# Feed-forward up projection: the raw weights' last product moved to the fourth place, and GpSimd's tables held back while VectorE makes its sums

## The chip, the core and the metric

One core of a Trainium2 chip runs the whole program. The metric is device time in microseconds (us) of one execution. Of the kernel before, three executions took 1297.13, 1298.35 and 1299.34 us; their median, 1298.35 us, is the time that the changed kernel is compared with.

## The reference, cut to what matters

The program computes one transformer block with a gated linear attention mixer and a convolutional gated feed-forward part, and then a second block (attention and delta-rule mixers, and 32 experts of which each token uses two). Everything is float32, with 256 tokens and a model width of 1024. The change touches only the feed-forward part of the first block:

```python
def conv_ffn(x, w_up, conv_w, conv_b, w_down):
    s = x.shape[1]
    u = x @ w_up                                   # [256, 1024] x [1024, 2 * 2816]
    u_pad = jnp.pad(u, ((0, 0), (CONV_WIDTH - 1, 0), (0, 0)))
    u = sum(u_pad[:, j:j + s] * conv_w[j] for j in range(CONV_WIDTH)) + conv_b
    gate, up = jnp.split(u, 2, axis=-1)
    return (jax.nn.silu(gate) * up) @ w_down       # [256, 2816] x [2816, 1024]
```

## The kernel before, in words

**How the up projection is tiled.** The hidden width of 2816 is cut into 22 tiles of 128 gate columns and 128 up columns. Each tile is a matrix product split two by two in three directions: the 256 tokens into halves, the 1024 inputs into a top and a low half, and the columns into gate and up. A scheme in Strassen's manner makes it from seven products of 128 x 512 by 512 x 128 instead of eight. Each product is four TensorE matmuls in the program and eight in the trace (float32 takes two passes). The profile calls the line of all of them L712.

**The seven products of tile i, in the order before.** X (raw gate weights, written to the PSUM bank `UP_X`); the corner, which belongs to tile i-1 and is added onto bank `UP_Q`; Y (raw weights, bank `UP_Y`); X1 (a table, added onto `UP_X`); Q (a table, bank `UP_Q`); X2 (a table, added onto `UP_X`); Z (raw up weights, bank `UP_Z`). Tile 0 has no corner. After each of X, X1 and X2 ScalarE copies bank `UP_X` to SBUF (copies 0, 1 and 2, lines L1380, L1386, L1388), and the next product that writes that bank waits for the copy. There is one such bank, so that X of the next tile waits for copy 2 of this one. VectorE adds the copies to banks `UP_Q`, `UP_Y` and `UP_Z` (L1774), does the convolution's taps (L1737) and the gate's multiplication (L1748); ScalarE does the first tap (L1364) and the silu (L1370).

**Where the operands come from.** SyncE's queue (SP) loads a tile's weights, 1 MB, into one of two buffers (L448). Load i waits until tile i-2 has used the buffer: for TensorE's product count `up_done` and for the four tables of that tile. After loads 4, 7, 10, 13 and 16 a 2 MB chunk of another matrix (`w_ada`, L228) goes through the same queue. GpSimd (POOL) makes four sums of weight quarters for each tile, the tables (L2267 to L2272), and in the down projection four for each of its 11 pairs of tiles (L2280 to L2285). VectorE makes four sums of token quarters once, `tok_sums` (L1726 to L1731), and four for each pair of the down projection (L1756 to L1759).

**The down projection** makes 7 products of 128 x 128 by 128 x 512 for each pair (L781): p1, p2, p6, p7, p5, p4, p3. Of pair 0, p6 waits for VectorE's sums and GpSimd's tables, and p4 for a small VectorE step, `modulation(1, 7, 8)` (L1767), which stands behind the sums of pair 1 in VectorE's order. The first such step, `modulation(0, 1, 0)`, frees the bank that Z of tile 0 writes.

All orders are written out by hand; each engine runs its list in order, and semaphores tie the lists together.

Of the kernel before, what the change touches and what calls it, by code (L numbers as in the profile page):

```python
# [104 lines left out]
def build_program(nc, I, out):  # L105

    ctx = ExitStack()
    with ctx:
# [271 lines left out]
        for group, steps in (  # L380
# [5 lines left out]
            ("pool_tables", (("vr_tables", 8), ("up_tables", 4 * FT), ("down_tables", 4 * NPAIR), ("x2_part", 3))),  # L386
# [43 lines left out]
        def _(sp):  # L430
# [100 lines left out]
        def _(pe):  # L531
# [190 lines left out]
            def ff_up(i, s, loaded, first=False):  # L722
# [16 lines left out]
                pe.wait_ge(*after("up_tables", i * 4 + 2))  # L739
                pe.wait_ge(S["up_copied"], i * 3 + 1)  # L740
                up_product(UP_X, up_t[s][:, 1], tok_sums[:, 1], False)
                if not first:
                    pe.wait_ge(S["up_added"], i * 4)
                up_product(UP_Q, up_t[s][:, 0], tok_sums[:, 0], True)
                if first:
                    pe.wait_ge(*after("tok_sums", 3))
                pe.wait_ge(*after("up_tables", i * 4 + 3))
# [10 lines left out]
            def ff_down(p):  # L758
# [7 lines left out]
                for name in PART:  # L766
# [27 lines left out]
            pe.wait_ge(*after("up_tables", 4 * FT))  # L794
# [505 lines left out]
        def _(act):  # L1300
# [71 lines left out]
            def up_copies(i, s, first=False, taps_free=None):  # L1372
# [249 lines left out]
        def _(dve):  # L1622
# [105 lines left out]
            dve.tensor_tensor(tok_sums[:, 1], quarters[1][1], tok_sums[:, 0], ALU.subtract).then_inc(made("tok_sums"), 1)  # L1728
            dve.tensor_tensor(tok_sums[:, 2], quarters[1][1], quarters[0][1], ALU.subtract).then_inc(made("tok_sums"), 1)
            dve.wait_ge(*after("tok_sums", 3))  # L1730
            dve.tensor_tensor(tok_sums[:, 3], tok_sums[:, 1], quarters[1][0], ALU.subtract).then_inc(made("tok_sums"), 1)  # L1731
# [29 lines left out]
            def modulation(group, b, plain):  # L1761

                dve.wait_ge(S["ada_turned"], group + 1)
                turned = bank(b).rearrange("p (n r) -> p n r", n=16)[:, :, 0]
                bias = col("b_ada")[:, 16 * group:16 * group + 16]
                for n0 in (0, 8):
                    m = dve.scalar_tensor_tensor(out=mod[:, 16 * group + n0:16 * group + n0 + 8], in0=turned[:, n0:n0 + 8],  # L1767
                                                 scalar=0.0 if n0 == plain else 1.0, in1=bias[:, n0:n0 + 8], op0=ALU.add, op1=ALU.add)
                m.then_inc(S["mod_ready"], 1)

            modulation(0, 1, 0)
# [4 lines left out]
            def up_adds(i, s, first=False):  # L1776
# [11 lines left out]
                dve.wait_ge(S["up_done"], i * 7 + 6)  # L1788
# [456 lines left out]
        def _(pool):  # L2245
# [15 lines left out]
            pool.wait_ge(S["rows_scaled"], 4)  # L2261
            for i in range(FT):
# [4 lines left out]
                pool.tensor_tensor(t[:, 0], w[:, 0:4, 1, :], w[:, 4:8, 1, :], ALU.add).then_inc(made("up_tables"), 1)  # L2267
                pool.wait_ge(*after("up_tables", 4 * i + 1))
# [108 lines left out]
```

## Time and profile before

| | |
|---|---|
| median of 3 runs | 1298.35 us (1297.13 to 1299.34) |
| the profiled execution's own time | 1298.34 us |
| its span on the core | 1296.5 us |
| busy in the span: TensorE matmul | 1145.4 us (88%) |
| VectorE | 487.1 us (38%) |
| ScalarE | 246.1 us (19%) |
| GpSimd | 237.2 us (18%) |
| mean granted TensorE clock | 0.971 of full speed |

The up projection stands between about 170 and 318 us of the span, the down projection between 318 and 390 us. In the trace a row is a group of like instructions: start, length, engine, line, operation, output<-inputs with shapes, and in brackets how long the engine had been idle and whose work ended that. PE is TensorE's matmul, PEld its weight load, DVE VectorE, ACT ScalarE, POOL GpSimd, SPq SyncE's queue. A matmul's length is its latency. Matmuls are pipelined and start much closer together than that.

### The profile page before, as it was taken

Reading aid. Unit: us, or ns where it says so; the run is one execution under the profiler, and the core shown is the slowest. Engines: PE = TensorE matmul, PEld = TensorE weight load, DVE = VectorE, ACT = ScalarE, POOL = GpSimd, SP = SyncE. Lnnn points to the kernel's source line nnn. Section 1 sums busy time; section 2 is a strip of 40 time slices with the busy share of each in tenths; the row PEclk is TensorE's granted clock in tenths of the full one; section 3 lists DMA queues with packets and bytes.
Section 4 is the critical chain, followed back from the end, with each engine's and each line's share of the span. In section 5 each row is a group of like instructions: output and inputs, shape, how many; then the busy total and the mean of one; then the engine's idle time right before and its main releaser. Section 6 shows DMA issues by size and latency. Waiting matters only on the chain.

```text
span 1296.5 us, 22618 instructions
## 1 busy us (share of the span) xinstructions
PE 1145.4 (88%) x8992; PEld 801.6 (62%) x8993; DVE 487.1 (38%) x1093; ACT 246.1 (19%) x561; POOL 237.2 (18%) x160
## 2 busy tenths in 40 slices
PE   7999989998999999999998999877887667788766
PEld 5646489998448878888858985533444323444333
DVE  2213155567663623442574312422332212333224
ACT  1302023333002211054201201211111101111112
POOL 0550066888770000000102000300000000000000
PEclk9999999999999999999998999989999879999889
DMA  9338737653347454431444096599999999699996
GB/s 333 139 129 316 276 123 292 240 214 129 134 142 240 130 195 146 179 131 65 103 153 136 1 349 239 205 380 403 431 429 428 428 429 428 259 429 429 429 428 264
DMA packets 88169, 334.86 MB, mean 258 GB/s; under 512 B 24353, under 2 KB 25505, under 8 KB 72882
## 3 DMA queue, kind: packets, MB, share of 16 engines
q1 hardware_dynamic: 72850, 331.94, 65.2%
q10 hardware_dynamic: 15264, 2.13, 1.0%
q8 instruction: 41, 0.67, 0.2%
q14 instruction: 14, 0.11, 0.0%
HBM read 332.22 MB, written 1.84 MB: 258 GB/s over the span
## 4 chain that ended last, share of the span: by engine, by line
PE 72%; DMA 17%; DVE 4%; issue 4%; ACT 1%; SPq 1%; POOL 0%; DVEq 0%
PE ps L544 18%; DMA main<-in_w_up 11%; PE ps L1211 9%; PE ps L712 9%; PE ps L781 5%; PE ps L554 4%; PE ps L598 4%; PE ps L1228 3%; DMA main<-in_w_gate 3%; PE ps L1097 2%; DMA main<-in_l_ffn_w_up 2%; PE ps L1191 2%; PE ps L1164 1%; PE ps L974 1%; DMA main<-in_l_gla_w_in 1%
## 5 line engine op out<-in xcount | busy, mean ns | idle before, releaser
L1211 PE MATMUL ps<-main 128*32 128x256 f32 x2176 | 176.9, 414 | 79.2 <-issue 38.0
L544 PE MATMUL ps<-main 128*128 128x256 f32 x1088 | 239.0, 381 | 0.6 <-DMA main<-in_l_gla_w_in 0.6
L544 PEld LDWEIGHTS ps<-main 128*128 128x128 f32 x1088 | 207.1, 191 | 32.6 <-issue 3.4
L1211 PEld LDWEIGHTS ps<-main 128*32 128x32 f32 x2176 | 90.8, 119 | 164.5 <-issue 110.3
L712 PE MATMUL ps<-main 128*128 128x128 f32 x1232 | 141.9, 278 | 5.1 <-DMA main<-in_l_ffn_w_up 2.8
L712 PEld LDWEIGHTS ps<-main 128*128 128x128 f32 x1232 | 140.1, 194 | 7.0 <-issue 4.5
L2176 DVE TENSOR_TENSOR main<-main,ps 64x256 f32<-64x256 f32 x34 | 14.4, 423 | 200.9 <-ACT main L1575 125.5
L781 PE MATMUL ps<-main 128*128 128x512 f32 x154 | 68.2, 605 | 3.6 <-DVE main L1759 3.6
L1228 PE MATMUL ps<-main 128*32 128x256 f32 x1088 | 65.8, 381 | 5.1 <-ACT main L1581 4.0
L1888 DVE SCALAR_TENSOR_TENSOR main<-ps,cols,main 128x255 f32<-128x255 f32 (+2 forms) x72 | 33.0, 480 | 69.7 <-ACT main L1437 68.0
L554 PE MATMUL ps<-main 128*128 128x512 f32 x128 | 55.6, 594 | 1.1 <-DVE main L1971 0.6
L781 PEld LDWEIGHTS ps<-main 128*128 128x128 f32 x154 | 29.7, 194 | 41.4 <-issue 36.7
L1164 PE MATMUL ps<-main 128*32 128x256 f32 x560 | 42.5, 389 | 12.0 <-DMA main<-in_w_up 8.3
L1575 ACT ACTIVATE main<-ps 64x256 f32<-64x256 f32 x34 | 12.8, 377 | 210.4 <-PE ps L1211 210.4
L1228 PEld LDWEIGHTS ps<-main 128*32 128x32 f32 x1088 | 36.2, 109 | 25.5 <-issue 11.7
L2295 POOL TENSOR_TENSOR main<-main,consts 128x2048 f32<-128x2048 f32 x1 | 4.5, 4533 | 247.5 <-DVE main L1968 247.5
L2267 POOL TENSOR_TENSOR main<-main 128x512 f32<-128x512 f32 x22 | 28.6, 1299 | 109.3 <-DVE main L1640 76.1
L598 PE MATMUL ps<-main 128*128 128x512 f32 x112 | 48.2, 592 | 0.0
L1191 PE MATMUL ps<-main 128*128 128x512 f32 x96 | 43.4, 595 | 2.8 <-DVE main L2187 2.8
L1586 ACT ACTIVATE main<-ps 32x256 f32<-32x256 f32 x68 | 25.4, 374 | 104.9 <-PE ps L1228 104.1
L2185 DVE TENSOR_TENSOR main<-ps,main 32x256 f32<-32x256 f32 x68 | 28.8, 423 | 43.6 <-PE ps L1228 42.5
L554 PEld LDWEIGHTS ps<-main 128*128 128x128 f32 x128 | 24.1, 190 | 31.0 <-issue 29.2
(385 smaller groups left out, 1422.4 us busy)
## 6 DMA issues: line engine op xcount, KB each, us to landing
main<-in_w_up SPq DMA_DIRECT2D x32, 2048.0 KB, 23.5
main<-in_w_gate SPq DMA_DIRECT2D x32, 2048.0 KB, 19.0
main<-in_w_down SPq DMA_DIRECT2D x32, 2048.0 KB, 26.4
main<-in_w_in SPq DMA_DIRECT2D x15, 2048.0 KB, 7.7
main<-in_w_ada SPq DMA_DIRECT2D x12, 2048.0 KB, 9.9
main<-in_l_ffn_w_up SPq DMA_DIRECT2D x22, 1024.0 KB, 4.8
main<-in_l_gla_w_in SPq DMA_DIRECT2D x6, 2048.0 KB, 13.7
main<-in_l_ffn_w_down SPq DMA_DIRECT2D x11, 1024.0 KB, 4.9
```

The source lines that it names most:

```text
L544: m = pe.matmul(ps[:, banks[m4 // 2], (m4 % 2) * T:(m4 % 2) * T + T], chunk8(n)[:, k, m4 * P:(m4 + 1) * P], act[:, k, :], start=(k == 0), ...
L554: m = pe.matmul(ps[:, banks[j], :], act[:, k, j * P:(j + 1) * P], chunk8(n)[:, k, :], start=(k == 0), stop=(k == KD - 1))
L598: m = pe.matmul(ps[:, b, :], left[:, k, :], right[:, k, :], start=(start and k == 0), stop=(stop and k == 3), skip_group_check=True)
L712: m = pe.matmul(ps[:, b, 0:P], left[:, k, :], right[:, k, :], start=(first and k == 0), stop=(k == 3), skip_group_check=True)
L781: m = pe.matmul(ps[:, PART_BANK[name], :], left, right, start=(p == 0), stop=(p == NPAIR - 1))
L1164: m = pe.matmul(ps[q * SLOTS:(q + 1) * SLOTS, 4, 0:T], sel[s][:, j, :], x[:, j, q * T:(q + 1) * T], start=(j == 0), stop=(j == 1))
L1191: m = pe.matmul(ps[:, 2 * j + half, :], selgT[:, j * P:(j + 1) * P], rows[:, half * HALF:(half + 1) * HALF], start=False, stop=False, skip ...
L1211: m = pe.matmul(ps[q * SLOTS:(q + 1) * SLOTS, 5, 0:T], rows[:, k, :], w, start=(k == 0), stop=(k == KD - 1))
L1228: m = pe.matmul(ps[q * SLOTS:(q + 1) * SLOTS, 7, 0:T], hidT[:, kt % 2, (kt // 2) * SLOTS:(kt // 2 + 1) * SLOTS], dw[:, kt, q * T:(q + 1) * ...
L1888: m = dve.scalar_tensor_tensor(out=dnT[:, n, gap:], in0=ps[:, b, (n % 2) * T:(n % 2 + 1) * T - gap], scalar=col("dn_conv")[:, tap * 24 + n ...
L2185: dve.tensor_tensor(dst[a:a + SLOTS, part], ps[rows, 7, 0:T], gt_row2[rows, part], ALU.mult).then_inc(S["yexp_ready"], 1)
L2267: pool.tensor_tensor(t[:, 0], w[:, 0:4, 1, :], w[:, 4:8, 1, :], ALU.add).then_inc(made("up_tables"), 1)
```

## The change

Four things are changed.

1. **Order of the products.** Z moves from the seventh to the fourth place: X, corner, Y, Z, X1, Q, X2. X2 is now the tile's last product. In tile 0 the order is X, Y, X1, Z, Q, X2.
2. **The load's wait.** The raw weights are used up after Z, so SP waits for a product count that is lower by 2. ScalarE's and VectorE's counts follow the new order.
3. **Start of the stage.** VectorE makes sums 0 and 1, then `modulation(0, 1, 0)`, then sums 3 and 2. GpSimd waits for all four before it makes the tables of tile 1.
4. **End of the stage.** GpSimd makes the down tables of pair 0 right behind the up tables of tile 1, and those of pair 1 wait for VectorE's sums of pair 0. The counts of the tables are in two groups each (ahead, later) for that.

```diff
@@ up projection, SyncE
                 if used is not None:
-                    sp.wait_ge(S["up_done"], 7 * used - 1)
-                    sp.wait_ge(*after("up_tables", 4 * used))
+                    sp.wait_ge(S["up_done"], 7 * used - 3)
+                    sp.wait_ge(*up_tables(4 * used))
@@ ff_up, TensorE
                     up_corner(i - 1, 1 - s)
+                    pe.wait_ge(S["up_added"], i * 4 - 1)
                 up_product(UP_Y, gate_low[s], h_low[:, :, 0:P], True)
-                if first:
+                if not first:
+                    up_product(UP_Z, up_low[s], tok_sums[:, 3], True)
+                else:
                     pe.wait_ge(*after("tok_sums", 2))
...
                 pe.wait_ge(S["up_copied"], i * 3 + 1)
                 up_product(UP_X, up_t[s][:, 1], tok_sums[:, 1], False)
-                if not first:
+                if first:
+                    pe.wait_ge(*after("tok_sums", 3))
+                    pe.wait_ge(S["mod_ready"], 1)
+                    up_product(UP_Z, up_low[s], tok_sums[:, 3], True)
+                else:
                     pe.wait_ge(S["up_added"], i * 4)
                 up_product(UP_Q, up_t[s][:, 0], tok_sums[:, 0], True)
...
                 pe.wait_ge(S["up_copied"], i * 3 + 2)
                 up_product(UP_X, up_t[s][:, 2], tok_sums[:, 2], False)
-                if first:
-                    pe.wait_ge(*after("tok_sums", 4))
-                    pe.wait_ge(S["mod_ready"], 1)
-                up_product(UP_Z, up_low[s], tok_sums[:, 3], True)
@@ up_copies, ScalarE (copies 1 and 2)
-                act.wait_ge(S["up_done"], i * 7 + 3)
+                act.wait_ge(S["up_done"], i * 7 + 4)
...
-                act.wait_ge(S["up_done"], i * 7 + 5)
+                act.wait_ge(S["up_done"], i * 7 + 6)
@@ up_adds, VectorE (the add of Z, behind the add of Q)
-                dve.wait_ge(S["up_done"], i * 7 + 6)
+                dve.wait_ge(S["up_done"], i * 7 + 4)
@@ VectorE, behind tok_sums 0 and 1
+            modulation(0, 1, 0)
+            dve.wait_ge(*after("tok_sums", 2))
+            dve.tensor_tensor(tok_sums[:, 3], tok_sums[:, 1], quarters[1][0], ALU.subtract).then_inc(made("tok_sums"), 1)
             dve.tensor_tensor(tok_sums[:, 2], quarters[1][1], quarters[0][1], ALU.subtract).then_inc(made("tok_sums"), 1)
-            dve.wait_ge(*after("tok_sums", 3))
-            dve.tensor_tensor(tok_sums[:, 3], tok_sums[:, 1], quarters[1][0], ALU.subtract).then_inc(made("tok_sums"), 1)
...
-            modulation(0, 1, 0)
@@ GpSimd (the loop bodies became functions; one wait is new in the down tables)
                 if p == 1:
                     pool.wait_ge(S["up_done"], UP_LAST)
+                    pool.wait_ge(*after("down_sums", 1))
...
+            pool.wait_ge(S["rows_scaled"], 4)
+            up_part_tables(0)
+            pool.wait_ge(*after("tok_sums", 4))
+            up_part_tables(1)
+            down_part_tables(0)
+            for i in range(2, FT):
+                up_part_tables(i)
+            for p in range(1, NPAIR):
+                down_part_tables(p)
```

TensorE, in the loop over the tiles, from Q of one tile to X of the next, before (each L712 MATMUL row with x3 behind one alone is a product of four matmuls; x7 is that and one more product):

```order
L712 MATMUL ps<-main 128x128 [waits up_added]
L712 MATMUL ps<-main 128x128 x3
L747 REGISTER_ALU
L748 REGISTER_ALU [waits pool_tables]
L712 MATMUL ps<-main 128x128 [waits up_copied]
L712 MATMUL ps<-main 128x128 x7
L728 ISA [waits up1_loaded]
L712 MATMUL ps<-main 128x128 [waits up_copied]
L712 MATMUL ps<-main 128x128 x3
```

And the same stretch now (L712 has become L720):

```order
L720 MATMUL ps<-main 128x128 [waits up_added]
L720 MATMUL ps<-main 128x128 x3
L762 REGISTER_ALU
L763 REGISTER_ALU [waits pool_tables]
L720 MATMUL ps<-main 128x128 [waits up_copied]
L720 MATMUL ps<-main 128x128 x3
L736 ISA [waits up1_loaded]
L720 MATMUL ps<-main 128x128 [waits up_copied]
L720 MATMUL ps<-main 128x128 x3
```

Behind X2 stood Z (the last four of x7); now X of the next tile follows X2 directly, and its first row waits for `up_copied`, the count of ScalarE's copies.

GpSimd at the start of the up projection, before (tables of tiles 0, 1 and the first of tile 2):

```order
L2267 TENSOR_TENSOR main<-main 128x512 [waits up0_loaded,rows_scaled]
L2269 TENSOR_TENSOR main<-main 128x512 [waits pool_tables]
L2270 TENSOR_TENSOR main<-main 128x512
L2272 TENSOR_TENSOR main<-main 128x512 [waits pool_tables]
L2267 TENSOR_TENSOR main<-main 128x512 [waits up1_loaded]
L2269 TENSOR_TENSOR main<-main 128x512 [waits pool_tables]
L2270 TENSOR_TENSOR main<-main 128x512
L2272 TENSOR_TENSOR main<-main 128x512 [waits pool_tables]
L2267 TENSOR_TENSOR main<-main 128x512 [waits up_done,up0_loaded]
```

And now, from the tables of tile 1 on (`x2_sums` is the semaphore of `tok_sums`):

```order
L2279 TENSOR_TENSOR main<-main 128x512 [waits up1_loaded,x2_sums]
L2281 TENSOR_TENSOR main<-main 128x512 [waits pool_tables]
L2282 TENSOR_TENSOR main<-main 128x512
L2284 TENSOR_TENSOR main<-main 128x512 [waits pool_tables]
L2295 TENSOR_TENSOR main<-main 128x512 [waits down0_loaded]
L2296 TENSOR_TENSOR main<-main 128x512
L2298 TENSOR_TENSOR main<-main 128x512 [waits pool_tables]
L2300 TENSOR_TENSOR main<-main 128x512 [waits pool_tables]
L2279 TENSOR_TENSOR main<-main 128x512 [waits up_done,up0_loaded]
```

Tile 1's tables have a wait for VectorE that they had not, and the four down tables of pair 0 stand ahead of tile 2's. They stood behind tile 21's.

## Rows read from the trace of the kernel before

**Rows 1.** The chain that ended last, 170 to 330 us: start, length, what.
```profile
172.43 1.64 DVE main L1728
...
200.41 7.77 DMA main<-in_l_ffn_w_up
...
322.86 1.28 DVE main L1759
```
**Rows 2.** Timeline of TensorE alone, 166 to 330 us.
```profile
187.61 19.02 PE L712 MATMUL ps<-main 128*128 128x128 f32 x168
208.30 19.04 PE L712 MATMUL ps<-main 128*128 128x128 f32 x168 [1.67 <-DMA main<-in_l_ffn_w_up]
...
266.87 51.52 PE L712 MATMUL ps<-main 128*128 128x128 f32 x456 [0.32 <-DMA main<-in_l_ffn_w_up]
```
**Rows 3.** Timeline of the ends of two tiles, 213.9 to 222.3 us.
```profile
213.97 0.28 ACT L1388 ACTIVATE main<-ps 128x128 f32<-128x128 f32 x1 [1.51 <-PE ps L712]
...
220.23 0.28 ACT L1388 ACTIVATE main<-ps 128x128 f32<-128x128 f32 x1 [1.51 <-PE ps L712]
...
220.54 0.29 DVE L1774 TENSOR_TENSOR ps<-main,ps 128x128 f32<-128x128 f32 x1 [0.35 <-ACT main L1388]
...
221.11 0.33 SPq L448 DMA_DIRECT2D main<-in_l_ffn_w_up  x1
```
**Rows 4.** Timeline behind a wait for a load, 207.5 to 210.5 us.
```profile
208.29 2.31 PEld L712 LDWEIGHTS ps<-main 128*128 128x128 f32 x20 [1.85 <-issue]
...
209.49 0.28 ACT L1380 ACTIVATE main<-ps 128x128 f32<-128x128 f32 x1 [3.13 <-PE ps L712]
```
**Rows 5.** The page's DMA issues: count, KB each, us to landing.
```profile
main<-in_l_ffn_w_up SPq DMA_DIRECT2D x22, 1024.0 KB, 4.8
```
**Rows 6.** Timeline of the start, 160 to 200 us.
```profile
169.35 1.27 POOL L2272 TENSOR_TENSOR main<-main 128x512 f32<-128x512 f32 x1
...
170.81 1.59 DVE L1726 TENSOR_TENSOR main<-main 128x512 f32<-128x512 f32 x1
...
174.12 11.67 PE L712 MATMUL ps<-main 128*128 128x128 f32 x88 [2.13 <-DVE main L1728]
```
**Rows 7.** VectorE's groups by form, 10 to 110 us: busy us, mean ns, idle.
```profile
L1658 DVE TENSOR_TENSOR main<-main 128x512 f32<-128x512 f32 x1 | 0.7, 692 | 0.0
```
**Rows 8.** Busy by stretch: PE, PEld, DVE, ACT, POOL; then PEclk.
```profile
163.80:167.20 3.40, 1.75 (x63) 1.48 (x51) 1.58 (x3) 0.02 (x1) 1.57 (x2) 1.00 0.90 345
170.70:174.00 3.30, 1.28 (x10) 0.97 (x8) 3.23 (x4) 0.28 (x1) 3.22 (x3) 1.00 0.02 5
174.10:177.40 3.30, 3.28 (x15) 3.28 (x16) 3.27 (x3) 0.28 (x1) 2.77 (x2) 0.50 0.00 0
...
324.30:327.60 3.30, 3.30 (x4) 1.37 (x5) 2.71 (x9) 0.42 (x1) 1.04 (x1) 0.50 0.00 0
```
**Rows 9.** Timeline of the end of the stage, 300 to 345 us.
```profile
316.56 0.28 ACT L1388 ACTIVATE main<-ps 128x128 f32<-128x128 f32 x1 [1.51 <-PE ps L712]
...
318.66 1.88 PE L781 MATMUL ps<-main 128*128 128x512 f32 x4
...
320.36 1.23 DVE L1757 TENSOR_TENSOR main<-main 128x128 f32<-128x128 f32 x1
...
324.06 1.77 DVE L1737 SCALAR_TENSOR_TENSOR main<-ps,cols,main 128x255 f32<-128x255 f32 x4
...
324.19 21.27 PE L781 MATMUL ps<-main 128*128 128x512 f32 x45 [3.65 <-DVE main L1759]
...
326.31 0.43 DVE L1748 TENSOR_TENSOR main<-main 128x256 f32<-128x256 f32 x1 [0.48 <-ACT main L1370]
326.65 0.29 DVE L1756 TENSOR_TENSOR main<-main 128x128 f32<-128x128 f32 x1
...
327.71 0.23 DVE L1767 SCALAR_TENSOR_TENSOR small<-ps,cols 128x8 f32<-128x8 f32 x2
328.13 0.19 PEld L781 LDWEIGHTS ps<-main 128*128 128x128 f32 x1 [0.24 <-DVE small L1767]
```

More of the change, by code:

```diff
@@ L403, in after, with up_tables, down_tables @@
             return S[group], before + n
+        def up_tables(n):
+            return after("up_tables_ahead", n) if isinstance(n, int) and n <= 8 else after("up_tables_later", n - 8)
+        def down_tables(n):
+            return after("down_tables_ahead", n) if n <= 4 else after("down_tables_later", n - 4)
         sem("x_loaded", "consts_loaded", "cols_loaded", "alpha_loaded", "dve_step", "act_step",
@@ L745, in ff_up @@
                 if first:
[L746 to L747 removed]
+                    pe.wait_ge(*after("tok_sums", 4))
+                pe.wait_ge(*up_tables(i * 4 + 3))
                 pe.wait_ge(S["up_copied"], i * 3 + 2)
                 up_product(UP_X, up_t[s][:, 2], tok_sums[:, 2], False)
[L750 to L753 removed]
             PART = ("p1", "p2", "p6", "p7", "p5", "p4", "p3")
@@ L774, in ff_down @@
                         pe.wait_ge(*after("down_sums", p + 1))
-                        pe.wait_ge(*after("down_tables", 4 * p + 4))
+                        pe.wait_ge(*down_tables(4 * p + 4))
                     if name == "p4" and p == 0:
@@ L793, in _ @@
             pe.wait_ge(S["up_added"], 4 * FT - 2)
-            pe.wait_ge(*after("up_tables", 4 * FT))
+            pe.wait_ge(*up_tables(4 * FT))
             up_corner(FT - 1, 1)
@@ L1728, in _, with modulation @@
             dve.tensor_tensor(tok_sums[:, 1], quarters[1][1], tok_sums[:, 0], ALU.subtract).then_inc(made("tok_sums"), 1)
+            def modulation(group, b, plain):
+                dve.wait_ge(S["ada_turned"], group + 1)
+                turned = bank(b).rearrange("p (n r) -> p n r", n=16)[:, :, 0]
+                bias = col("b_ada")[:, 16 * group:16 * group + 16]
+                for n0 in (0, 8):
+                    m = dve.scalar_tensor_tensor(out=mod[:, 16 * group + n0:16 * group + n0 + 8], in0=turned[:, n0:n0 + 8],
+                                                 scalar=0.0 if n0 == plain else 1.0, in1=bias[:, n0:n0 + 8], op0=ALU.add, op1=ALU.add)
+                m.then_inc(S["mod_ready"], 1)
+            modulation(0, 1, 0)
+            dve.wait_ge(*after("tok_sums", 2))
+            dve.tensor_tensor(tok_sums[:, 3], tok_sums[:, 1], quarters[1][0], ALU.subtract).then_inc(made("tok_sums"), 1)
             dve.tensor_tensor(tok_sums[:, 2], quarters[1][1], quarters[0][1], ALU.subtract).then_inc(made("tok_sums"), 1)
-            dve.wait_ge(*after("tok_sums", 3))
-            dve.tensor_tensor(tok_sums[:, 3], tok_sums[:, 1], quarters[1][0], ALU.subtract).then_inc(made("tok_sums"), 1)
             def ff_conv(done, s, i, taps):
@@ L1759, in ff_sums @@
                 dve.tensor_tensor(u[:, 3, :], b[:, 0:P], u[:, 1, :], ALU.subtract).then_inc(made("down_sums"), 1)
[L1761 to L1769, printed above, removed]
-            modulation(0, 1, 0)
             def add_product(s, c, part, b, op=ALU.add):
@@ L2260, in _, with up_part_tables @@
                 pool.tensor_tensor(top[:, 4:8, :], t2, top[:, 4:8, :], ALU.subtract).then_inc(made("vr_tables"), 1)
-            pool.wait_ge(S["rows_scaled"], 4)
-            for i in range(FT):
+            def up_part_tables(i):
                 w, t = up_w[i % 2], up_t[i % 2]
@@ L2266, in _, with down_part_tables @@
                     pool.wait_ge(S["up_done"], 7 * i - 6)
-                pool.tensor_tensor(t[:, 0], w[:, 0:4, 1, :], w[:, 4:8, 1, :], ALU.add).then_inc(made("up_tables"), 1)
-                pool.wait_ge(*after("up_tables", 4 * i + 1))
-                pool.tensor_tensor(t[:, 1], t[:, 0], w[:, 0:4, 0, :], ALU.subtract).then_inc(made("up_tables"), 1)
-                pool.tensor_tensor(t[:, 2], w[:, 0:4, 0, :], w[:, 0:4, 1, :], ALU.subtract).then_inc(made("up_tables"), 1)
-                pool.wait_ge(*after("up_tables", 4 * i + 2))
-                pool.tensor_tensor(t[:, 3], w[:, 4:8, 0, :], t[:, 1], ALU.subtract).then_inc(made("up_tables"), 1)
-            for p in range(NPAIR):
+                pool.tensor_tensor(t[:, 0], w[:, 0:4, 1, :], w[:, 4:8, 1, :], ALU.add).then_inc(made("up_tables_later"), 1)
+                pool.wait_ge(*up_tables(4 * i + 1))
+                pool.tensor_tensor(t[:, 1], t[:, 0], w[:, 0:4, 0, :], ALU.subtract).then_inc(made("up_tables_later"), 1)
+                pool.tensor_tensor(t[:, 2], w[:, 0:4, 0, :], w[:, 0:4, 1, :], ALU.subtract).then_inc(made("up_tables_later"), 1)
+                pool.wait_ge(*up_tables(4 * i + 2))
+                pool.tensor_tensor(t[:, 3], w[:, 4:8, 0, :], t[:, 1], ALU.subtract).then_inc(made("up_tables_later"), 1)
+            def down_part_tables(p):
                 w, t = down_w[p % 3], down_t[p % 2]
```

18 lines of the change are left out of this document (9 added, 9 removed).

## The prediction

> **What bounds the kernel now.** I read the chain of waits first. From 170 to 390 us it is TensorE's products, broken at a few places: two of VectorE's sums at the start, the landing of a weight tile four times, and VectorE's sums again at the end [rows 1]. So what a change does here is the sum of TensorE's gaps in this stage. The timeline of TensorE alone gives them: 2.13 us before X1 of tile 0 [rows 6], 1.67 us before tile 5 and 0.32 before tile 14, with 0.33 and 0.46 before tiles 8 and 11 between them [rows 2], and 3.65 us before p6 [rows 9]. Inside the tiles there is none. Copy 2 of one tile starts 6.26 us after that of the tile before [rows 3], 0.894 us for each of seven products. The stages behind start from the end of this one, so I let a shift of it through to the end in full.
>
> **Step 1: the new order puts a copy between two products (A).** Before, Z stood between X2 and the next tile's X. Now X follows X2 and writes the same bank, which copy 2 has to leave first. Nothing else is queued on TensorE that could go ahead, since its list is in order. The parts: copy 2 starts when X2's result is seen, at 220.23, and takes 0.28 us [rows 3]. A release takes about 0.06 us to a running product: L1728 ends at 172.43 + 1.64 = 174.07 [rows 1], and the product starts at 174.12 [rows 6]. From the start of an X that had to wait to its result being seen: 208.30 [rows 2] to 209.49 [rows 4], 1.19 us. So X's result is seen 0.28 + 0.06 + 1.19 = 1.53 us behind X2's, where an undisturbed product follows after 0.894. The wait costs 0.64 us. X of tile 1 and of tiles 3 to 21 pay it, 20 in all; tile 2 has 64 short matmuls of another matrix ahead of it, which cover the copy. A = 20 x 0.64 = +12.8 us. Bounds: the start of TensorE behind a wait costs about 0.10 of this (1.19 against 1.09 for eight matmuls in a stream), and without it A is 20 x 0.54 = 10.8; with 0.70, if ScalarE is a little late at the copy, 14.
>
> The row shows the weight load of the waiting X starting at 208.29, 0.01 us before its matmul, and not ahead of the wait [rows 4]. The Trainium skill ("TensorE: Matmul & The Clock Gate", "Architectural detail: the array is 16× 32×32, not 1× 128×128") says that TensorE can pull a weight load ahead of matmuls in flight. By that rule X's weights would be there when the copy ends and the sum would take the lower bound of A; by the row it takes 12.8. The row decides, as its wait stands in front of the load.
>
> **Step 2: the loads start earlier (C).** SP issues a load at the end of Z: 221.11 against copy 2 at 220.23, one product later [rows 3]. It lands 4.8 us later as a median [rows 5], within a tile's 6.26; behind the 2 MB chunk it takes 7.77 us [rows 1], and TensorE stands. Now the load waits for X1, two products earlier (1.79 us) than Z stood, and A makes each tile longer, so a load behind a chunk has some 8.05 + 1.3 us before its X. 7.77 fits. GpSimd's tables could hold the load instead, as SP waits for those of tile i-2 too. Their four operations of 1.27 us take 5.1 us a tile [rows 6], under the 6.9 us of a tile; they start when a load lands, earlier than now, so they are done before that tile's X1. What goes is read from the whole stretch: tiles 2 to 13 take 187.61 to 266.87, 79.26 us [rows 2], where 12 x 6.26 is 75.1. C = -4.2 us, of which 2.8 is the idle time named above and the rest starts behind waits and tables that came late with the loads. Bounds: -2.8 to -4.4.
>
> **Step 3: the start (D).** The first sum, L1726, starts at 170.81 and takes 1.59 us, the second 1.64 [rows 6, 1], beside GpSimd's tables of tile 1. A VectorE sum of this shape with GpSimd idle takes 0.69 us [rows 7]. GpSimd's tables of tile 0 end at 169.35 + 1.27 = 170.62 [rows 6], before the first sum, and it waits now until all four are made. So the second sum ends at about 170.81 + 2 x 0.69 + 0.04 = 172.23, and X1 starts at 172.29 instead of 174.12: -1.83 us. The modulation (0.2 to 0.4 us, [rows 9]) and sum 3 follow by 173.3, when X1 is over; sum 2 by 174.0, before X2 at 175.1. GpSimd then makes tile 1's first two tables by 176.6, and X1 of tile 1 comes at about 179.9. The down tables of pair 0 move tile 2's to 184.3, where they stood already. The granted clock was 0.50 of full speed (1.2 of 2.4 GHz) from 174.1 to 177.4, behind a stretch in which TensorE was busy for 1.28 of 3.30 us [rows 8]: 88 matmuls from 174.12 took 11.67 us, where 11 products of 0.894 are 9.83 [rows 6]. With the gap down to 0.3 us I expect no such drop: another -1.8. D = -3.6. Bounds: -1.8 (drop stays) and -3.7.
>
> The Trainium skill ("SBUF — State Buffer", "Who interferes with whom") says that a VectorE operation with two SBUF inputs and a GpSimd operation lock each other out for a whole instruction. The row agrees, 1.59 us beside GpSimd against 0.69 alone. The same rule speaks against step 4: it says that a table which has started is waited for in full.
>
> **Step 4: the end (E).** Counted from the start of copy 2 of tile 21, 316.56 before [rows 9]. That copy comes one product later now, +0.89, as X2 is last. The last corner waits for the add of Q behind the copy: 0.31 + 0.29 [rows 3] + 0.06 + 1.19 = 1.85 to its result, +0.96 over a stream. p1 started at 2.10 [rows 9], so now at 2.10 - 0.89 + 0.96 = 2.17. VectorE adds the corner by 2.14 and makes pair 0's sums with GpSimd silent at 0.29 each [rows 9], done at 3.2 instead of 324.14 - 316.56 = 7.6; p1 and p2 are over only at 2.17 + 1.72 = 3.9 (0.43 us a matmul, from the 4 in 1.88 [rows 9]). So p6 does not wait: the 3.65 us are gone. What is late next: p6, p7 and p5 end at 6.5, and p4 waits for the modulation, behind convolution, multiplication and pair 1's sums on VectorE. The tables of pair 1 now start at 3.25 and run to 8.4, beside them. Convolution from 3.15; the multiplication starts 2.25 later (324.06 to 326.31 [rows 9]), at 5.4, and gets through at the next table's end, 6.05. Beside GpSimd a sum takes 1.23 [rows 9]: the first to 7.3, the second to 8.6, the other two and the modulation by 9.55. p4 started at 328.13 - 316.56 = 11.57. So E = 9.55 + 0.89 - 11.57 = -1.1 us at full clock. But TensorE is idle from 6.5 to 9.55, about 3.05 us. Gaps of 3.65 and 2.13 us were followed by half clock, one of 1.7 us was not (1.75 of 3.40 us busy, [rows 8]); before, the drop lay over p6 to p5 and was over at 327.6, by then p4 had not started. A drop behind the new gap costs up to 1.8 us, the price at the start. I take E = +0.4, nearer to the drop. Bounds: -1.1 and +0.7.
>
> **The sum.** 12.8 - 4.2 - 3.6 + 0.4 = +5.4 us. The profiled execution took 1298.34 us for its span of 1296.5, and the median of the runs is 1298.35, so the two are the same base: 1298.35 + 5.4 = 1303.7 us. The bounds together: 10.8 - 4.4 - 3.7 - 1.1 = +1.6 and 14 - 2.8 - 1.8 + 0.7 = +10.1. It is unlikely that all lie at one end, and half-clock stretches further on may shift by one either way, 1.8 us.
>
> **The rivals.** A measurement of this kernel tells about 0.2%, 2.6 us, from no change.
>
> *The copy is hidden (faster).* Place: between X2 and X of the next tile. If the release reached TensorE while X2's results still drain, or the tile's rhythm gave it room, the wait would cost nothing, and -4.2 - 3.6 - 1.1 - 0.9 (the corner's wait hidden too) = -9.8: 1288.5 us. It decides from 0.37 us a tile downwards ((4.2 + 3.6 - 0.4) / 20); above that the change loses. For it speaks only that no tile shows a gap now; against it that the copy alone, 0.28, with a product's drain before it, is a fact of the rows, and that VectorE sees the copy 0.31 us after its start [rows 3]. 6%.
>
> *The gains all come and the wait is at its lower bound (no change).* +1.6 to +2.6: 1300.4 us. For it: weights pulled ahead, no clock drop at the end. Against: the row of the waiting weight load. 13%.
>
> *The start keeps its clock drop or GpSimd becomes the bound.* Against a drop: the gap shrinks to 0.3 us. For GpSimd as the bound: four down tables (5.1 us) stand ahead of tile 2, and load 4 waits for tile 2's tables at about 189.4, so that a chain of late tables could follow; against it, load 4 has until 198. D at -1.8 and C at -2.8 give +8.6: 1306.9 us. 17%.
>
> *The waits don't change at all*, because TensorE already stood for the copy somewhere: against it, 6.26 us a tile are 56 matmuls without a gap. Below 1%, in the case of no change.
>
> **Numbers.** The forecast, 1301.0 to 1306 with 1303.7 at its centre, has 63%. Faster by over 0.2% (below 1295.7): 6%. Within 0.2% (to 1301.0): 14%. Slower: 80%. The range that holds 8 in 10: 1300.4 to 1307.2 us.
>
> **What the changed profile would show.** Step 1: idle time of TensorE ahead of L720 put down to ScalarE's copy L1399, about 20 times, 0.5 us each in the row (which counts from the modelled end of the matmul) or less, and tiles 6.9 us apart. Step 2: no wait of TensorE for `in_l_ffn_w_up`, loads issued at the end of X1. Step 3: L1737 and L1739 at 0.69 us, X1 of tile 0 at 172.3, PEclk 1.00 behind it. Step 4: no wait of p6, one of about 3 us of p4 on the modulation, and sums of pair 1 at 1.2 us. The prediction is wrong if tiles stay at 6.26 to 6.5 us apart, or if X of the next tile starts before the copy ends.

## The result and the profile after

The changed kernel is slower: 1305.72 us in the median of 7 runs (1303.59 to 1307.31) against 1299.34 us for 7 runs of the kernel before. The ratio is 1.0041, with a 95% interval of 1.0026 to 1.0056: 5.3 us (3.4 to 7.3) of 1299. The two medians themselves lie 6.4 us apart, which is inside that interval. Forecast were 1303.7 us, 1300.4 to 1307.2, and +5.4 us. The profiled execution took 1303.59 us, with a span of 1301.8.

Who TensorE waited for between 158 and 400 us (total us, times, longest):

```profile
PE ps L720 <- ACT main L1399: 7.4, 20, 0.5
PE ps L792 <- DVE small L1747: 2.9, 1, 2.9
...
PE ps L720 <- DVE ps L1786: 0.7, 1, 0.7
PE ps L720 <- DVE main L1739: 0.3, 1, 0.3
```

The first row is new, and it is the change's cost: 20 waits for copy 2. The waits for loads, for p6 and of 2.1 us for the second sum [rows 2, 6, 9] are gone. The last row, 0.3 us, is what is left of the wait for the second sum. New are also the second row (p4 on the modulation) and the third (the last corner on the add of Q).

TensorE's timeline, against [rows 2, 6, 9] of before:

```profile
169.08 2.26 PE L720 MATMUL ps<-main 128*128 128x128 f32 x16 [0.16 <-DVE main L1657]
171.63 3.84 PE L720 MATMUL ps<-main 128*128 128x128 f32 x32 [0.29 <-DVE main L1739]
...
184.23 6.52 PE L720 MATMUL ps<-main 128*128 128x128 f32 x56
191.12 6.52 PE L720 MATMUL ps<-main 128*128 128x128 f32 x56 [0.37 <-ACT main L1399]
...
266.86 6.52 PE L720 MATMUL ps<-main 128*128 128x128 f32 x56 [0.37 <-ACT main L1399]
...
322.26 1.16 PE L720 MATMUL ps<-main 128*128 128x128 f32 x8 [0.70 <-DVE ps L1786]
...
323.70 4.46 PE L792 MATMUL ps<-main 128*128 128x512 f32 x10
331.10 14.43 PE L792 MATMUL ps<-main 128*128 128x512 f32 x33 [2.94 <-DVE small L1747]
```

A tile starts 6.885 us after the one before (184.23 to 191.12 to 266.86, twelve tiles), where it was 6.26: 0.625 us more. The bracket says only 0.37, as it counts from the modelled end of the last matmul: a row of 56 is 6.52 us long, 0.26 more than the 6.26 from one tile's start to the next in a stream, and 0.26 + 0.37 is the 0.63. Read such a wait by the distance of the starts.

The end of one tile, against [rows 3, 4]:

```profile
218.33 0.28 ACT L1399 ACTIVATE main<-ps 128x128 f32<-128x128 f32 x1 [1.51 <-PE ps L720]
...
218.66 6.33 PEld L720 LDWEIGHTS ps<-main 128*128 128x128 f32 x56 [0.56 <-ACT main L1399]
218.66 6.52 PE L720 MATMUL ps<-main 128*128 128x128 f32 x56 [0.37 <-ACT main L1399]
...
219.86 0.28 ACT L1391 ACTIVATE main<-ps 128x128 f32<-128x128 f32 x1 [0.94 <-PE ps L720]
```

X starts 0.33 us after copy 2 does, and its result is seen at 219.86, 1.53 us behind X2's. The weight load (PEld) waits with its matmul, though this tile's weights had landed by 214.69, when GpSimd started on them.

The start, against [rows 6, 8]. The first three rows are the timeline, the last two the busy time by stretch (PE, PEld, DVE, ACT, POOL, then PEclk):

```profile
170.16 0.69 DVE L1737 TENSOR_TENSOR main<-main 128x512 f32<-128x512 f32 x1
...
170.89 0.69 DVE L1739 TENSOR_TENSOR main<-main 128x512 f32<-128x512 f32 x1
...
173.01 1.27 POOL L2279 TENSOR_TENSOR main<-main 128x512 f32<-128x512 f32 x1 [2.72 <-DVE main L1754]
```
```profile
170.00:173.40 3.40, 3.11 (x25) 2.75 (x25) 3.07 (x8) 0.28 (x1) 0.68 (x2) 1.00 0.02 5
173.50:176.90 3.40, 2.94 (x27) 2.78 (x25) 0.49 (x2) 0.55 (x2) 3.32 (x4) 1.00 0.63 188
```

The sums take 0.69 us with GpSimd silent, and the granted clock is 1.00 from 170.0 to 176.9.

The table splits four profiled executions, of 1298.34, 1295.56, 1303.59 and 1306.15 us in its order, into three stretches: X of tile 0 to p1 (up projection), p1 to the last down product, and from there to the end. Starts are first and last starts of the lines L712 and L781, or what they became; the last column is the span less the last product's start.

| kernel | X to p1 | p1 to last | X to last | behind |
|---|---|---|---|---|
| before | 149.0 | 71.2 | 220.2 | 906.6 |
| before, again | 147.3 | 72.5 | 219.8 | 904.7 |
| changed | 154.6 | 68.9 | 223.5 | 909.2 |
| changed, again | 154.6 | 70.5 | 225.1 | 909.7 |

### The profile page after: what moved, and what is told of

Read it like the earlier page. It is cut to its first block, busy times and chain, and to the rows that moved or that the text cites. A ratio compares the mean times of both kernels' runs of the same rounds, so it can differ in the third digit from the quotient of the medians.

```text
span 1301.8 us, 22639 instructions
## 1 busy us (share of the span) xinstructions
PE 1149.1 (88%) x8992; PEld 801.3 (62%) x8993; DVE 477.5 (37%) x1093; ACT 245.8 (19%) x561; POOL 233.3 (18%) x160
## 3 DMA queue, kind: packets, MB, share of 16 engines
q10 hardware_dynamic: 15264, 2.13, 1.0%
## 4 chain that ended last, share of the span: by engine, by line
PE 74%; DMA 14%; DVE 4%; issue 4%; ACT 2%; SPq 1%; POOL 0%; DVEq 0%; ACTq 0%
PE ps L552 18%; PE ps L720 11%; PE ps L1222 10%; DMA main<-in_w_up 8%; DMA main<-in_w_gate 5%; PE ps L792 4%; PE ps L562 4%; PE ps L606 4%; PE ps L1239 3%; PE ps L1108 2%; PE ps L1202 2%; PE ps L1175 1%; PE ps L985 1%; DMA main<-in_l_gla_w_in 1%; DMA main<-in_l_gla_w_out 1%
## 5 line engine op out<-in xcount | busy, mean ns | idle before, releaser
L1222 PE MATMUL ps<-main 128*32 128x256 f32 x2176 | 182.2, 424 | 77.0 <-issue 39.7
L552 PEld LDWEIGHTS ps<-main 128*128 128x128 f32 x1088 | 207.2, 191 | 32.2 <-issue 3.4
L720 PE MATMUL ps<-main 128*128 128x128 f32 x1232 | 144.1, 277 | 8.6 <-ACT main L1399 7.4
L720 PEld LDWEIGHTS ps<-main 128*128 128x128 f32 x1232 | 139.4, 192 | 13.3 <-ACT main L1399 10.6
L1239 PE MATMUL ps<-main 128*32 128x256 f32 x1088 | 65.8, 381 | 5.0 <-ACT main L1592 3.5
L1175 PE MATMUL ps<-main 128*32 128x256 f32 x560 | 42.5, 389 | 12.8 <-DMA main<-in_w_up 8.3
L792 PEld LDWEIGHTS ps<-main 128*128 128x128 f32 x154 | 29.1, 190 | 39.6 <-issue 35.6
L1586 ACT ACTIVATE main<-ps 64x256 f32<-64x256 f32 x34 | 12.8, 377 | 213.6 <-PE ps L1222 213.6
L1786 DVE TENSOR_TENSOR ps<-main,ps 128x128 f32<-128x128 f32 x88 | 23.9, 294 | 58.4 <-PE ps L720 29.2
```

The lines of the kernel that those rows point to most:

```text
L552: m = pe.matmul(ps[:, banks[m4 // 2], (m4 % 2) * T:(m4 % 2) * T + T], chunk8(n)[:, k, m4 * P:(m4 + 1) * P], act[:, k, :], start=(k == 0), ...
L720: m = pe.matmul(ps[:, b, 0:P], left[:, k, :], right[:, k, :], start=(first and k == 0), stop=(k == 3), skip_group_check=True)
L792: m = pe.matmul(ps[:, PART_BANK[name], :], left, right, start=(p == 0), stop=(p == NPAIR - 1))
L1175: m = pe.matmul(ps[q * SLOTS:(q + 1) * SLOTS, 4, 0:T], sel[s][:, j, :], x[:, j, q * T:(q + 1) * T], start=(j == 0), stop=(j == 1))
L1222: m = pe.matmul(ps[q * SLOTS:(q + 1) * SLOTS, 5, 0:T], rows[:, k, :], w, start=(k == 0), stop=(k == KD - 1))
L1239: m = pe.matmul(ps[q * SLOTS:(q + 1) * SLOTS, 7, 0:T], hidT[:, kt % 2, (kt // 2) * SLOTS:(kt // 2 + 1) * SLOTS], dw[:, kt, q * T:(q + 1) * ...
```

## The experiments

Ratios are to the kernel before, over its runs on the same chip. Since a whole run scatters by several us, each verdict rests on a stretch of the profile and the ratio only frames it. There is one profile of each experiment; the table above shows by how much two profiles of one kernel can differ: by 1.7 us in X to p1 and 1.6 in p1 to last. "X to p1" and "X to last" are meant as in the table, and the changed kernel's are 154.6 and 223.5 us, of the first profile.

**Two banks for X.** X, X1 and X2 of odd tiles go to bank 7, so each use of `UP_X` becomes `UP_X[s]`, with s = 1 in odd tiles.

```diff
-        UP_X, UP_Y, UP_Z, UP_Q = 3, 2, 1, 6
+        UP_X, UP_Y, UP_Z, UP_Q = (3, 7), 2, 1, 6
...
-                    pe.wait_ge(S["up_copied"], i * 3)
+                    pe.wait_ge(S["up_copied"], i * 3 - 3)
```

> The changed kernel, but X, X1 and X2 of odd tiles are written to PSUM bank 7, which is free in this stage, and X waits only for copy 2 of the tile before last. Order, loads, tables and sums stay as changed. If the wait of X for copy 2 is what the new order costs (0.63 us for each of 20 tiles), the tiles come 6.26 us apart again, TensorE has no wait for ScalarE's copy, and the time is 12.5 us under the changed kernel, about 7 us under the kernel before (1292). If TensorE is held by something else in the new order (GpSimd's tables, VectorE's adds, restarts that any order would have), tiles stay near 6.9 us apart and the time stays about 5 us over the kernel before.

Measured: 1296.16 us, ratio 0.9974 (0.9957 to 0.9991): 3.4 us under the kernel before, where 7 were expected. TensorE's timeline has 20 tiles in one row:

```profile
187.13 128.01 PE L720 MATMUL ps<-main 128*128 128x128 f32 x1120
315.84 1.16 PE L720 MATMUL ps<-main 128*128 128x128 f32 x8 [0.70 <-DVE ps L1786]
```

X to last is 213.5 us, 10.0 under the changed kernel; X to p1 is 144.7, 9.9 under it. Expected were 12.5. The tiles do run without a wait for a copy, but 1120 matmuls take 128.0 us here; the same row is 125.7 us long in the run with Q last and the modulation early (below), where no tile waits. So taking the bank's wait away gives 9.9 us of the 12.5, and some 2.6 us come back inside the loop. The timeline of one tile shows where, by who reads TensorE's results:

```profile
251.54 0.49 DVE L1786 TENSOR_TENSOR ps<-main,ps 128x128 f32<-128x128 f32 x2 [0.95 <-ACT main L1399]
252.12 0.28 ACT L1391 ACTIVATE main<-ps 128x128 f32<-128x128 f32 x1 [0.31 <-PE ps L720]
253.16 0.30 DVE L1786 TENSOR_TENSOR ps<-main,ps 128x128 f32<-128x128 f32 x1 [0.76 <-PE ps L720]
...
258.52 0.28 ACT L1391 ACTIVATE main<-ps 128x128 f32<-128x128 f32 x1 [0.31 <-PE ps L720]
```

X of the next tile is seen at 252.12. The corner behind it is seen at 253.16, 1.04 us later, where one product takes 6.26 / 7 = 0.89. X to X is 6.40 (258.52 - 252.12), so 0.14 more a tile, 2.7 over the 19 tiles 3 to 21 (tile 2's corner, read 0.89 behind its X, does not wait). TensorE's matmuls, looked at one by one behind this tile, start 0.11 us apart, but the corner's first starts 0.15 behind the last of X (258.36) and its second 0.21 behind that (258.57). The corner waits for VectorE's add of Q, which stands behind copy 2 (the first row, released by it): too short a pause to show as idle time. That the pause is the corner's is a fact of the rows; that it is this wait is read from them, as no run takes it away alone with two banks.

**The order alone.** The kernel before with parts 1 and 2 of the change only.

```diff
-                    sp.wait_ge(S["up_done"], 7 * used - 1)
+                    sp.wait_ge(S["up_done"], 7 * used - 3)
...
+                if not first:
+                    up_product(UP_Z, up_low[s], tok_sums[:, 3], True)
...
                 pe.wait_ge(S["up_copied"], i * 3 + 1)
                 up_product(UP_X, up_t[s][:, 1], tok_sums[:, 1], False)
```

> The kernel before with only the products' order and the load's wait changed; GpSimd's tables and VectorE's sums stay in their old order (so Z of tile 0 waits for the fourth sum, about 1.6 us more at the start). Theory: +12.6 for the copies, -4.2 for the loads, +1.6 at the start, about +0.5 at the end: 10.5 us over the kernel before (1310), and 5 over the changed kernel. If the moves of the tables and sums gain nothing, this one is equal to the changed kernel, 5 to 6 us over the kernel before (1305).

Measured: 1308.37 us, ratio 1.0056 (1.0034 to 1.0079); X to last 231.1 us, 10.9 over the kernel before, where 10.5 were expected. The sum came out, its terms less well: X of tile 0 to X of tile 2 takes 4.4 us more than before (193.76 - 171.49 against 187.61 - 169.72), where about 2.2 were expected (1.6 and one copy), and p1 to last is 1.8 us shorter, where 0.5 more was expected. At the start TensorE waits for the second sum, as before, and now for the modulation too, and the 24 matmuls behind that run at half clock (0.50 from 179.5 to 182.9):

```profile
175.95 1.16 PE L712 MATMUL ps<-main 128*128 128x128 f32 x8 [2.20 <-DVE main L1729]
179.54 5.46 PE L712 MATMUL ps<-main 128*128 128x128 f32 x24 [2.43 <-DVE small L1768]
```

**The tables alone.** The changed kernel with the products and the load's wait as before.

```diff
-                    sp.wait_ge(S["up_done"], 7 * used - 3)
+                    sp.wait_ge(S["up_done"], 7 * used - 1)
...
-                if not first:
-                    up_product(UP_Z, up_low[s], tok_sums[:, 3], True)
...
                 up_product(UP_X, up_t[s][:, 2], tok_sums[:, 2], False)
...
+                up_product(UP_Z, up_low[s], tok_sums[:, 3], True)
```

> The changed kernel with the products' order and the load's wait as before (Z last); only the tables, sums and the modulation are moved. Theory: 3.6 us less at the start (sums at 0.69 us, no half clock behind them), 0.3 to 2 less at the end, the four waits for loads as before: about 5 us under the kernel before (1294). If the moves are worth only the idle time at the start, 1.8 us under it (1297.5). If they gain nothing, equal to it.

Measured: 1297.63 us, ratio 0.9989 (0.9969 to 1.0010): 1.4 us less, where 5 were expected, and inconclusive by itself. X to last is 214.5 us, 5.7 under the kernel before, with the waits for loads still there (3.3 us, 4 times). Behind the last product, though, this execution took 912.0 us, 5.4 more than the first profile of before.

**Q last.** The changed kernel in the order X, corner, Y, X1, Z, X2, Q. The load starts at the same count, and Q covers copy 2.

```diff
                 up_product(UP_X, up_t[s][:, 1], tok_sums[:, 1], False)
...
+                up_product(UP_Z, up_low[s], tok_sums[:, 3], True)
...
                 pe.wait_ge(S["up_copied"], i * 3 + 2)
                 up_product(UP_X, up_t[s][:, 2], tok_sums[:, 2], False)
+                if not first:
+                    pe.wait_ge(S["up_added"], i * 4)
+                up_product(UP_Q, up_t[s][:, 0], tok_sums[:, 0], True)
```

> The changed kernel with another order of the products: X, corner, Y, X1, Z, X2, Q. The raw weights' last product is Z in the fifth place, at the count at which the load is issued in the changed kernel, and Q stands between X2 and the next X, so that copy 2 is covered. VectorE adds Z before Q. Theory: the loads' 4.2, the start's 3.6 and 0.5 to 1.5 us at the end are all gained and no copy is paid: 8 to 9 us under the kernel before (1291), tiles 6.26 us apart with no wait for in_l_ffn_w_up. If the early load is worth nothing by itself, 5 under it, as with the tables alone.

Measured: 1294.85 us, ratio 0.9954 (0.9936 to 0.9972): 6.0 us under the kernel before, where 8 to 9 were expected. X to p1 is 142.2 us, 12.4 under the changed kernel and 3.5 under the tables alone.

```profile
174.36 10.09 PE L720 MATMUL ps<-main 128*128 128x128 f32 x88 [0.29 <-DVE main L1736]
...
186.26 19.02 PE L720 MATMUL ps<-main 128*128 128x128 f32 x168
205.53 106.64 PE L720 MATMUL ps<-main 128*128 128x128 f32 x952 [0.24 <-DMA main<-in_l_ffn_w_up]
```

17 tiles in 106.6 us are 6.27 a tile. One wait for a load is left, 0.24 us. The clock was halved behind the wait of p4 (0.54 from 321.4 to 324.7), so X to last, 212.7 us, has some 1.7 us of that in it. This pair is the test of step 1: two orders with the same early load, 20 waits for copy 2 in one and none in the other, 12.4 us apart.

**Q last, load late.** The same with SP's wait two products later.

```diff
-                    sp.wait_ge(S["up_done"], 7 * used - 3)
+                    sp.wait_ge(S["up_done"], 7 * used - 1)
```

> Q last as run alone (modulation late), but SP waits for the tile's last product before it reloads the buffer, as in the kernel before. Theory: the four waits of tiles 5, 8, 11 and 14 for in_l_ffn_w_up come back, 1.7 and three of 0.3 to 0.8 us, and X of tile 0 to p1 takes 3.5 to 4.2 us more than the 142.2 of Q last. If the loads' gain came from elsewhere, 142.2 again.

Measured in one execution, of 1298.54 us: X to p1 146.5 us, 4.3 over Q last. The waits for loads are back, though not at the expected lengths: five of them, the longest 0.9 us, where four with one of 1.7 were expected.

```profile
PE ps L720 <- DMA main<-in_l_ffn_w_up: 3.0, 5, 0.9
```

**Start undone.** The changed kernel without GpSimd's wait for the four sums.

```diff
-            pool.wait_ge(*after("tok_sums", 4))
             up_part_tables(1)
```

> The changed kernel, but GpSimd makes tile 1's tables right behind tile 0's, beside VectorE's sums. Theory: the sums take 1.6 us each again, X1 of tile 0 starts 1.8 us later, behind a gap of some 2.1 us, and in the profile the granted clock may fall to 0.50 behind it, another 1.8: the stretch from X of tile 0 to the last down product rises from 223.5 to 225.3 or 227.1 us. If VectorE's sums are slow for another reason than GpSimd, they take 1.6 us in both and nothing changes.

Measured: 1308.93 us, ratio 1.0070 (1.0048 to 1.0093); X to last 225.4 us, 1.9 over the changed kernel, as in the milder of the two cases expected. The gap of 2.1 us did not come: TensorE waits 0.83 us for the second sum and 0.52 for the third, but X itself takes longer (16 matmuls in 2.87 us instead of 2.26), as the clock was already lowered ahead of it (0.79 from 168.0 to 171.4). The sums are slow again beside GpSimd:

```profile
172.99 1.60 POOL L2281 TENSOR_TENSOR main<-main 128x512 f32<-128x512 f32 x1
173.49 1.64 DVE L1739 TENSOR_TENSOR main<-main 128x512 f32<-128x512 f32 x1
```

**Copy twice.** One more ScalarE copy ahead of copy 2.

```diff
+                act.activation(spare, ps[:, UP_X, 0:P], ACT.Copy)
                 act.activation(up_parts[:, 2], ps[:, UP_X, 0:P], ACT.Copy).then_inc(S["up_copied"], 1)
```

> The changed kernel with one more ScalarE copy of the same size ahead of copy 2, from the same bank to an unused place. Theory: the release of X moves by the start distance of two ScalarE copies, 0.17 to 0.28 us, for 20 tiles: tiles 7.06 to 7.17 us apart instead of 6.885, 3.4 to 5.6 us more in all. If what holds X is TensorE's own drain or restart and not the copy, tiles stay 6.885 apart.

Measured: 1307.89 us, ratio 1.0062 (1.0040 to 1.0085). The copies start 0.18 us apart, and X starts 0.17 us later than without the second copy; tiles are 7.05 us apart:

```profile
192.97 0.28 ACT L1400 ACTIVATE main<-ps 128x128 f32<-128x128 f32 x1 [1.51 <-PE ps L721]
193.15 0.27 ACT L1401 ACTIVATE main<-ps 128x128 f32<-128x128 f32 x1
...
193.47 1.41 PEld L721 LDWEIGHTS ps<-main 128*128 128x128 f32 x12 [0.72 <-ACT main L1401]
```

X to p1 is 158.2 us, 3.6 over the changed kernel. X follows the copy, and TensorE's own drain does not set its start.

**The modulation early.** The changed kernel, with p4's modulation ahead of pair 1's sums.

```diff
             ff_sums(0)
+            modulation(1, 7, 8)
             ff_conv(FT - 1, 1, FT - 1, 2 * FT)
             ff_mul(FT - 1, 1, FT - 1)
             ff_sums(1)
-            modulation(1, 7, 8)
```

> The changed kernel with one VectorE step moved: modulation(1, 7, 8) right behind the sums of pair 0, instead of behind those of pair 1. Theory: p4 of pair 0 then waits for nothing, and the 2.94 us of the changed kernel's trace go; what could be late next is p6 of pair 1 (sums and tables about 331.1 us against its turn at 331.0, so at most 0.3). The stretch from X of tile 0 to the last product of the down projection falls from 223.5 to about 220.4 us, and the time by 3, or by up to 4.8 where a half clock followed the gap. If the end of the stage is set by GpSimd's tables of pair 1 rather than by the modulation, less than 1 us.

Measured: 1301.94 us, ratio 1.0017 (1.0003 to 1.0031). X to last is 221.9 us, 1.6 under the changed kernel and 3.2 under its second profile, which has a half clock in it: about half of the 3 and some two thirds of the 4.8 that were expected. The rows name a wait that I had put at 0.3 us at most:

```profile
330.00 1.31 POOL L2295 TENSOR_TENSOR main<-main 128x512 f32<-128x512 f32 x1
330.22 1.24 DVE L1781 TENSOR_TENSOR main<-main 128x128 f32<-128x128 f32 x1
...
331.38 1.35 DVE L1782 TENSOR_TENSOR main<-main 128x128 f32<-128x128 f32 x1
...
332.78 1.12 PE L792 MATMUL ps<-main 128*128 128x512 f32 x2 [1.38 <-DVE main L1782]
```

As p4 and p3 came earlier, GpSimd was released earlier to pair 2's tables, and these ran beside the last two sums of pair 1. The run that holds these tables (below) is the test of this.

**Q last and the modulation early**, both edits together.

> Q last (X, corner, Y, X1, Z, X2, Q) with modulation(1, 7, 8) right behind the sums of pair 0. Theory: the two gains add, as they lie at different places: the stretch from X of tile 0 to the last down product falls from 212.7 us (Q last alone, which had 1.7 us of half clock in it) to about 208 (207.5 to 209), and the time to 10 to 12 us under the kernel before (about 1288.5). If VectorE or GpSimd becomes the bound at the end once the gap goes, no more than with Q last alone, 5 to 6 under the kernel before.

Measured: 1289.49 us, ratio 0.9934 (0.9910 to 0.9958): 8.6 us under the kernel before, where 10 to 12 were expected. X to last is 209.3 us, just over the upper bound of 209, with the same 1.38 us in front of p6 of pair 1.

**Pair 2's tables held as well.** The last two edits stay, and one is added.

```diff
+                if p == 2:
+                    pool.wait_ge(*after("down_sums", 2))
                 if p >= 2:
```

> Q last and the modulation early, and GpSimd's tables of pair 2 wait for VectorE's sums of pair 1. In the trace with the modulation early alone, pair 2's tables started at once when p4 no longer waited, ran beside the last two sums of pair 1 (1.24 and 1.35 us instead of 0.29) and p6 of pair 1 waited 1.38 us. Theory: that wait goes, the stretch from X of tile 0 to the last down product falls from 209.3 to 207.9 us, the time by 1.4, to about 12 us under the kernel before (1288). If the sums are slow by themselves there, nothing changes; if tables of pair 2 are late now, p6 of pair 2 waits instead.

Measured: 1286.13 us, ratio 0.9913 (0.9893 to 0.9932), 11.3 us under the kernel before. X to last is 207.6 us, and TensorE has no wait in the down projection:

```profile
312.27 12.18 PE L789 MATMUL ps<-main 128*128 128x512 f32 x28
...
318.97 0.29 DVE L1778 TENSOR_TENSOR main<-main 128x128 f32<-128x128 f32 x1
319.18 0.28 DVE L1779 TENSOR_TENSOR main<-main 128x128 f32<-128x128 f32 x1
...
319.60 1.26 POOL L2294 TENSOR_TENSOR main<-main 128x512 f32<-128x512 f32 x1 [0.81 <-DVE main L1779]
```

It came out as expected (207.9 us, about 12 us), and this version beats both kernels.

**Both kernels once more**, for a second profile each.

> The kernel before, unchanged, for one more profile. X of tile 0 to the last down product 220.2 us again (218.4 if one of its two half clocks is missing); the stages behind it, 906.6 us in the first profile, may differ by some us. If they repeat within 1 us, the 2.6 us by which they were longer in the changed kernel belong to the change.

> The changed kernel, unchanged, for one more profile. X of tile 0 to the last down product 223.5 us, or 225.3 if a half clock follows the wait of p4; the stages behind it, 909.2 us in the first profile, vary as those of the kernel before do. If they are again 2.6 us longer than those of the kernel before, the change lengthens them.

The table above has them. The stages behind did not repeat within 1 us in the kernel before (906.6 and 904.7), so a single pair of profiles can't price them. In the second profile of the changed kernel the half clock did follow the wait of p4. Busy time by stretch, in the first profile and then in the second:

```profile
327.70:331.00 3.30, 0.45 (x2) 0.00 (x0) 3.23 (x7) 0.00 (x0) 2.44 (x2) 1.00 0.00 0
331.10:334.50 3.40, 3.40 (x8) 1.62 (x9) 1.28 (x2) 0.00 (x0) 1.27 (x1) 1.00 0.19 17
```
```profile
328.40:331.60 3.20, 0.27 (x2) 0.04 (x1) 3.04 (x6) 0.00 (x0) 2.21 (x2) 1.00 0.00 0
331.70:335.00 3.30, 3.30 (x5) 1.34 (x6) 0.44 (x2) 0.00 (x0) 0.43 (x1) 0.63 0.00 0
```

The same gap of 2.9 us, and p1 to last is 68.9 us in one and 70.5 in the other.

## Why the prediction was right, step by step

**Step 1 (A, +12.8).** Right. 1.53 us from X2 seen to X seen was forecast and measured; 20 waits, 0.625 us each by the starts, 12.5 in all, where 0.64 and 12.8 were forecast. Two orders with the same load differ by 12.4 us, and a longer copy moves X by as much. The lower bound, with the weights loaded ahead of the wait, did not come: the rows of the changed kernel show weight load and matmul of the waiting X starting together at 218.66. With two banks 9.9 us came back and not 12.5: there the corner is the next to wait for the same copy, by way of the add of Q, which I had taken to be early enough. By the rows that is some 2.7 us, not tested apart.

**Step 2 (C, -4.2).** Right. Tiles 2 to 13 take 266.86 - 184.23 = 82.6 us; twelve waits of 0.625 off leaves 75.1, where before it was 79.3: -4.1. The 0.625 is itself taken from these starts, so this says only that no other gap is left; the test is the early load undone alone, which cost 4.3. GpSimd's tables did not hold a load back: load 7, for one, is issued at 209.65, as X1's result is seen (209.66), where the tables that it also needs were made by 208.41.

**Step 3 (D, -3.6).** Right in the profile that it was made from: X of tile 0 to the short matmuls behind tile 1 took 185.72 - 169.72 = 16.0 us, and takes 182.35 - 169.08 = 13.3, with one wait for a copy in it, so D is -3.4. X1 starts 2.55 us behind X, forecast 172.29 - 169.72 = 2.57. The term that was sized wrong is the half clock, 1.6 us and not 1.8: the forecast set a row's length, 11.67, against 11 starts, 9.83, but the same 88 matmuls at full clock are a row of 10.09 us (in Q last). And the half clock is not in every execution at that place. In the second profile of before it fell earlier:

```profile
169.29 2.69 PE L712 MATMUL ps<-main 128*128 128x128 f32 x16
172.70 2.95 PE L712 MATMUL ps<-main 128*128 128x128 f32 x24 [0.72 <-DVE main L1728]
```

X took 2.69 us there instead of 2.26, the wait before X1 was 0.72 instead of 2.13, and X to p1 took 147.3 us instead of 149.0. So D lies between -1.7 and -3.4, and undoing the start cost 1.9.

**Step 4 (E, +0.4 with a half clock, -1.1 without).** The chain was right: p4 starts 9.49 us behind copy 2 of tile 21 (331.10 - 321.61), forecast 9.55, and 7.40 us behind p1, forecast 9.55 - 2.17 = 7.38; p6 does not wait. By the forecast's own count that is 9.49 + 0.89 - 11.57 = -1.2. Of the two cases, the first profile shows the one without the drop, and the second the one with it.

**The sum.** X to last: +3.3 us in the first pair of profiles, where 5.4 less the drop (1.5) is +3.9. With the drop, the second profile of the changed kernel is 4.9 over the first of the kernel before and 5.3 over its second, where +5.4 was forecast. The measured +5.3 over whole runs holds this and what the stages behind did. I had let a shift pass through them unchanged, and that assumption is not borne out. In the 14 profiles of this study they take from 904.7 to 912.1 us: 904.7 and 906.6 in the kernel before, 909.2 and 909.7 in the changed one. By the test that I had set (2.6 us longer again) the change lengthens them. Against it, the changed kernel with the modulation early, which has the whole change in it, takes 905.8, and the one with the old order of the products (the tables alone) 912.0. What sets them stays open. The same 6534 matmuls keep TensorE busy there for 775.2 us at a mean granted clock of 0.97 in the shortest of these stretches, and for 781.9 at 0.96 in the longest, so most of the difference lies in TensorE's own busy time; what lengthens it no run shows. That the total agrees with the forecast to 0.1 us is partly luck: in the first pair of profiles the stretch is 2.1 us short of the forecast and the stages behind add 2.6, and the medians themselves, 6.4 us apart, would put the forecast 1 us off (2.0 us by the time itself, 1305.72 against 1303.7).

**The rivals.** The hidden copy is refuted by the 20 waits. That the start keeps its clock drop is refuted in both profiles of the changed kernel (granted clock 1.00 behind X1 of tile 0), and GpSimd as the bound by TensorE having no wait for a table or a load. No change is refuted by the interval.

## What to carry to other kernels

Where one accumulator is read out several times in a tile, look for what stands between the last write and the next tile's first: moving an unrelated product out from there costs the drain of the last write, the copy and the restart, here 0.63 us a tile, where the bracket of the row says 0.37. Free the operand early by moving another product, so that an independent one (here Q) stays behind the last read: the same early load, and no wait for the copy. After a stall is taken away, look at what the faster engine releases: GpSimd started its next tables sooner and slowed the two sums that were awaited next, until it was held too.

## What the runs showed of the hardware

With GpSimd's operations back to back, VectorE's sums of two SBUF operands got one turn for each of them: 128 x 128 took 0.28 us with GpSimd silent and 1.24 to 1.35 beside it, ending 0.15 us behind the end of a GpSimd operation of 1.31 (331.46 against 331.31, modulation early).

The same gap of 2.9 us in TensorE was followed by a granted clock of 1.00 in one execution of the same kernel and by 0.63 over the next 3.3 us in another. Eight of the profiles have this gap: in five the clock behind it was 1.00 and p1 to last took 68.8 to 68.9 us, in three it was 0.54 to 0.64 and p1 to last took 70.5 to 70.6. That is 1.6 us of a kernel's time which no edit explains. Single runs of one kernel, the one before, lay between 1294 and 1306 us; this and the stages behind account for part of that, how much is not shown.
